# One log/exp table for ScalarE, loaded by hand, and two neighbouring norms taken as one, in a three-block fp32 model on one core

## The reference, cut to what matters

```python
def rmsnorm(x, g):
    return x * lax.rsqrt(jnp.mean(x * x, -1, keepdims=True) + RMS_EPS) * g          # RMS_EPS = 1e-6
def _layer_norm(x, g, b):
    mu = jnp.mean(x, -1, keepdims=True)
    var = jnp.mean(jnp.square(x - mu), -1, keepdims=True)
    return (x - mu) * lax.rsqrt(var + LN_EPS) * g + b                                # LN_EPS = 1e-5

def first_block(x, ...):
    ...                                       # S5 mixer
    out = (y * jax.nn.silu(gate)) @ sgu_w_out[j]
    x = x + out
    return rmsnorm(x, final_g)                # block 1's last norm
def second_block(x, ...):
    h = _layer_norm(x, ln_in_g, ln_in_b)      # block 2's first norm
    proj = h @ w_in[i]
    ...
```

## Time and profile before

| | before |
|---|---|
| median of 3 runs (lowest, highest) | 4123.22 us (4118.02, 4128.06) |
| the profiled execution's own time | 4112.57 us |
| its span | 4110.8 us |
| mean granted TensorE clock | 0.978 |
| TensorE busy (weight loads) | 95% (48%) |
| VectorE, ScalarE, GpSimd busy | 42%, 21%, 14% |
| DMA | 175.02 MB, 43 GB/s on average |

### The profile page before, as it was taken

How to read it: one execution, slowest core, us unless ns; L and a number is a source line. 1 busy time by engine, 2 the same in 40 slices (tenths; PEclk the granted TensorE clock), 3 DMA queues, 4 the chain that set the end, 5 groups by cost and what they waited for, 6 DMA issues and landing times.

```text
span 4110.8 us, 32365 instructions
## 1 busy us (share of the span) xinstructions
PE 3906.0 (95%) x12967; PEld 1982.8 (48%) x12967; DVE 1723.9 (42%) x2515; ACT 882.8 (21%) x1033; POOL 559.8 (14%) x605
## 2 busy tenths in 40 slices
PE   8999999999999999878999999999899999899998
PEld 4554444544345766443444444444355554444554
DVE  8576334333334441244533232323445553424432
ACT  2112111111552212342310000000323420321122
POOL 0343100121002220122111222122000000000000
PEclk9999999999999999999999999999999999999999
DMA  5323111111011110200111111111101001003101
GB/s 144 80 66 88 41 52 41 41 41 41 16 36 42 26 42 19 69 21 14 44 46 41 41 41 51 41 41 41 36 21 32 26 11 47 13 13 100 31 11 51
DMA packets 291233, 175.02 MB, mean 43 GB/s; under 512 B 24103, under 2 KB 281998, under 8 KB 290830
## 3 DMA queue, kind: packets, MB, share of 16 engines
q1 hardware_dynamic: 264736, 132.24, 11.8%
q0 software_dynamic: 9424, 22.30, 2.1%
q10 hardware_dynamic: 16926, 18.43, 1.4%
HBM read 159.72 MB, written 13.21 MB: 42 GB/s over the span
## 4 chain that ended last, share of the span: by engine, by line
PE 55%; ACT 2%; DVE 2%; issue 1%; DMA 0%; POOL 0%; ACTq 0%; DVEq 0%
PE products L326 23%; PE products L2934 8%; PE products L161 7%; PE products L2947 3%; PE others L3013 2%; PE products L2135 1%; PE products L179 1%; PE products L534 1%; PE products L2298 1%; PE others L2329 1%; PE products L2144 1%; PE products L3462 1%; PE products L3461 1%; PE others L1546 1%; PE others L3046 1%
## 5 line engine op out<-in xcount | busy, mean ns | idle before, releaser
L2934 PE MATMUL products<-normed,weights 128*128 128x512 f32 (+2 forms) x704 | 321.6, 607 | 5.0 <-DVE normed L520 5.0
L161 PE MATMUL products<-normed,weights 128*128 128x512 f32 x704 | 309.8, 600 | 8.4 <-DVE s_small L3673 4.0
L326 PE MATMUL products<-gate,s_small 128*128 128x512 f32 x704 | 313.0, 592 | 0.0
L326 PE MATMUL products<-work,s_small 128*128 128x512 f32 x544 | 243.3, 592 | 0.0
L326 PE MATMUL products<-normed,s_small 128*128 128x512 f32 x512 | 230.1, 592 | 2.3 <-DVE row L382 2.3
L344 POOL TENSOR_TENSOR s_small<-weights 128x512 f32<-128x512 f32 x60 | 77.3, 1288 | 1137.6 <-PE products L326 967.0
L356 ACT ACTIVATE s_small<-products 128x512 f32<-128x512 f32 x60 | 35.8, 597 | 860.9 <-PE products L326 860.9
L161 PEld LDWEIGHTS products<-normed,weights 128*128 128x128 f32 x704 | 134.0, 192 | 176.5 <-issue 164.8
L326 PEld LDWEIGHTS products<-gate,s_small 128*128 128x128 f32 x704 | 133.8, 190 | 168.4 <-issue 168.4
L326 PE MATMUL products<-normed,weights 128*128 128x512 f32 x448 | 203.6, 597 | 3.0 <-ACT normed L1077 3.0
L2934 PEld LDWEIGHTS products<-normed,weights 128*128 128x128 f32 (+2 forms) x704 | 126.4, 186 | 164.0 <-issue 162.0
(11 more groups left out here) (594 smaller groups left out, 6119.7 us busy)
## 6 DMA issues: line engine op xcount, KB each, us to landing
weights<-in_w_in_dram SPq DMA_DIRECT2D x83, 512.0 KB, 3.8
weights<-in_w_up_dram SPq DMA_DIRECT2D x32, 512.0 KB, 4.9
weights<-in_w_down_dram SPq DMA_DIRECT2D x32, 512.0 KB, 4.7
weights<-in_sgu_w_in_dram SPq DMA_DIRECT2D x24, 512.0 KB, 5.1
weights<-in_s_w_in_dram SPq DMA_DIRECT2D x16, 512.0 KB, 4.9
weights<-in_w_out_dram SPq DMA_DIRECT2D x24, 256.0 KB, 2.8
branch_scratch<-work POOLq DMA_DIRECT2D x8, 512.0 KB, 3.2
work<-branch_scratch POOLq DMA_DIRECT2D x64, 64.0 KB, 2.6
```

The source lines that it names most:

```text
L161: last = pe.matmul(out[0:cols, half * BANK:(half + 1) * BANK], slot(c, b, kt, cols)[:, k, :], acts[n][:, half * BANK:(half + 1) * BANK], s ...
L326: last = pe.matmul(bank, w[:, k * P:(k + 1) * P], moving[k], start=(k == 0 and n in (1, 3, 5)), stop=(k == KT // 2 - 1), skip_group_check= ...
L2934: last = pe.matmul(out[0:cols, half * BANK:(half + 1) * BANK], slot(c, f.b, kt, cols)[:, kk, :], acts[kk][:, half * BANK:(half + 1) * BANK ...
```

## The change

**By hand.** A class `Scalar` wraps ScalarE's queue. `logs()` loads the set `natural_log_exp_and_others` (set 6, which holds Ln and Exp) unless it is loaded already, and is called at 14 places in the code, most of them ahead of a wait. `activation()` calls it ahead of any Ln or Exp where no place did. For functions outside it (Silu and Sigmoid, for instance) the compiler still puts loads. [...] The program now has 95 loads: 40 of set 6, one of set 5, none of set 0, and the others as before.

**The joined norm.** The RMS norm between the blocks is gone. A class `Weighted` adds up gain times residual for the first seven tiles while the SGU's product is added to the residual (one VectorE pass of 128x1024 for each tile), and VectorE makes two 128x128 matrices: `last_mean`, the mean matrix with its rows scaled by the eighth tile's gain, and `little`, the mean matrix times LN_EPS. The layer norm takes its mean from the total and the eighth tile, subtracts it while it scales (`scalar_tensor_tensor` in place of `tensor_tensor`), and its mean of squares begins with `little` times the sum of the plain squares. `eps_both` is RMS_EPS·LN_EPS; one more constant is set on GpSimd at the start.

```diff
+class Scalar:
+    LOGS = (ACT.Ln, ACT.Exp)
+    ANY = (ACT.Copy, ACT.Identity, ACT.Square, ACT.Abs)
+    def logs(self):
+        if not self.has_logs:
+            self.act.preload_act_table_set("natural_log_exp_and_others")
+        self.has_logs = True
+    def finer_log(self):
+        self.act.preload_act_table_set("natural_log")
+        self.has_logs, self.fine_log = False, True
+    def activation(self, out, source, func, **kw):
+        if func in self.LOGS:
+            if func != ACT.Ln or not self.fine_log:
+                self.logs()
+        elif func not in self.ANY:
+            self.has_logs = False
+        ...
+        return self.act.activation(out, source, func, **kw)
+class Weighted:
+    def matrices(self, dve):
+        c.dve_chain.done(dve.tensor_scalar(self.last_mean, c.mean_mat[:, :], self.gain[:, KT - 1:KT], None, ALU.mult))
+        c.dve_chain.done(dve.tensor_scalar(self.little, c.mean_mat[:, :], LN_EPS, None, ALU.mult))
+    def collect(self, dve, m):
+        c.dve_chain.wait()
+        if m == 0:
+            c.dve_chain.done(dve.tensor_scalar(self.total, c.X[:, m, :], self.gain[:, m:m + 1], None, ALU.mult))
+            return
+        c.dve_chain.done(dve.scalar_tensor_tensor(self.total, c.X[:, m, :], self.gain[:, m:m + 1], self.total, ALU.mult, ALU.add),
+                         c.collected if m == KT - 2 else None)
+    def mean(self, pe, g, last_group):
+        out = start_group(c, pe, g)
+        pe.wait_ge(c.collected, self.collected)
+        ...                                   # 2 matmuls: mean_mat x total
+        taken(c, pe, last_group)
+        ...                                   # 2 matmuls: last_mean x X[7]
+    def before_squares(self, pe, out):
+        pe.wait_ge(sem, value)                # the eighth tile's square
+        ...                                   # 4 matmuls: little x (total of squares, last square)
@@ ln_phase
-            out = start_group(c, pe, g_mean)
-            for k in range(KT):
-                pe.wait_ge(c.normed, after + k + 1)
-                for h in range(HALVES):
-                    last = pe.matmul(out[:, h * BANK:(h + 1) * BANK], c.mean_mat[:, :], src[:, k, h * BANK:(h + 1) * BANK],
-        sum_squares(c, pe, g_sq, *squared)
+            weighted.mean(pe, g_mean, g_mean - 1)
+        sum_squares(c, pe, g_sq, *squared, weighted)
     def scalar(act):
+        act.logs() if weighted is None else act.finer_log()
...
-            ins = dve.tensor_tensor(dst[:, k, :], src[:, k, :], mean, ALU.subtract)
+                ins = dve.scalar_tensor_tensor(dst[:, k, :], src[:, k, :], weighted.gain[:, k:k + 1], mean, ALU.mult, ALU.subtract)
@@ fox_phase
+        act.logs()
         exponentials(0)
@@ residual_sums: collect(m) is sums.collect and then weighted.collect
@@ the program
-        norm = then(rms_phase(c, c.X, c.X, c.vec["final_g"], sums=sgu.sums))
-        norm = then(ln_phase(c, c.X, c.X, c.vec["ln_in_g_2"], c.vec["ln_in_b_2"], after=norm.normed))
+        norm = then(ln_phase(c, c.X, c.X, c.vec["ln_in_g_2"], c.vec["ln_in_b_2"], weighted=sgu.weighted))
```

More of the change, by code:

```diff
@@ L525, in rms_phase, with sum_squares @@
     return phase
-def sum_squares(c, pe, g, ready, used):
+def sum_squares(c, pe, g, ready, used, weighted=None):
     out = start_group(c, pe, g)
+    if weighted is not None:
+        weighted.before_squares(pe, out)
     for k in range(KT):
@@ L534, in sum_squares @@
             last = pe.matmul(out[:, h * BANK:(h + 1) * BANK], c.mean_mat[:, :], c.tmp[:, k % 2, h * BANK:(h + 1) * BANK],
-                             start=(k == 0), stop=(k == KT - 1))
+                             start=(k == 0 and weighted is None), stop=(k == KT - 1))
         last.then_inc(c.square_used if k < KT - 1 else c.group_done, 1)
@@ L551, in next_squares, with ln_phase @@
     return ready, used
-def ln_phase(c, src, dst, gain, bias, means=None, after=None, squares_next=False):
+def ln_phase(c, src, dst, gain, bias, means=None, squares_next=False, weighted=None):
     g_mean = c.plan.groups
@@ L1316, in square_pairs, with residual_sums, collect @@
     squares(len(pairs) - 1)
-def residual_sums(c, dve, pairs, sums, scale=None):
+def residual_sums(c, dve, pairs, sums, scale=None, weighted=None):
+    def collect(m):
+        if m >= 1:
+            sums.collect(dve, m)
+        if weighted is not None and m >= 0:
+            if m == 0:
+                weighted.matrices(dve)
+            weighted.collect(dve, m)
     for i, pair in enumerate(pairs):
         pair.add_all(dve, sums.src[:, 2 * i + 1, :], sums.src[:, 2 * i, :], scale,
-                     *((lambda m=2 * i - 1: sums.collect(dve, m), lambda m=2 * i: sums.collect(dve, m)) if i else ()))
+                     lambda m=2 * i - 1: collect(m), lambda m=2 * i: collect(m))
 def add_to_residual(c, dve, g, sums=None):
@@ L1525, in vector @@
                     ms.make(c, dve, name, a, m_ready)
-        residual_sums(c, dve, outs, sums)
+        residual_sums(c, dve, outs, sums, weighted=weighted)
     phase = Phase(loads=loads, tensor=tensor, scalar=scalar, vector=vector, gpsimd=gpsimd)
-    phase.sums = sums
+    phase.weighted = weighted
     return phase
```

58 lines of the change are left out of this document (51 added, 7 removed).

## The result

| | before | after |
|---|---|---|
| median of the runs (lowest, highest) | 4120.62 us (4110.50, 4128.06) | 4071.23 us (4064.20, 4071.61) |
| span of the profiled execution | 4110.8 us | 4069.6 us |
| mean granted clock | 0.978 | 0.980 |
| TensorE's idle time (span less busy) | 204.8 us | 177.1 us |

The ratio is 0.9875, 95% interval 0.9858 to 0.9892: about 51 us faster. Over all the timings of both kernels in this study (33 executions before, 8 after) the medians are 4121.3 and 4068.4 us, 52.9 apart. Two executions of the study, one of the kernel before (4263.78 us) and one of the variant heads_reload (5903.44 us), had a mean granted clock of 0.928 and 0.646 and are left out. The two profiled executions are only 41.2 apart; why is a question for the experiments.

What follows compares the result with a forecast made beforehand. TensorE, busy 3906.0 of 4110.8 us, was taken as the bound. Loads 27.9, joined norm 22.2, loss −1.3 and clock +3 made 52 us, taken from 4123.2 to give 4071; 8-in-10 range 4052 to 4095.

Steps and rivals of the forecast that it cites:

- (a): Seven norms, from the load phase's to the last: one exposed load less at each, 9.0 us gained.
- (b): Three attention heads and block 3's norms: two exposed loads less at each, 15.1 us together, two block 3 stalls capped at 4.9.
- R1: Rival: VectorE and GpSimd chains set the long stalls at heads and block 3; only 30 us gained, 4093; chance 0.15.
- (c): Block 3's 5.1 us stall at L3013 <- L3194: three loads less in ScalarE's chain, 3.8 us gained.
- (d): Joined norm between the blocks: fewer matmuls and waits, little matmuls covering the first square, one exposed load staying; 22.2 us gained.
- (e): Block 3's small Exp: its load, hidden by a wait before, now stands behind it; 1.3 us lost.
- (f): Half-clock stretches behind long stalls: shorter stalls give some time back, +3 us taken, bounds −6 and +10.
- R3: Rival: shorter stalls no longer end in half-clock stretches; eleven places gain 20.9 us in place of 3, 4053; chance 0.14.
- R2: Rival: a switch costs more than its load's row, exposed parts come back double; 80 us gained, 4043; chance 0.04.
- R4: Rival: the joint set's load is longer; at 5 us each the kernel is 65 us slower, 4188; chance 0.025.
- R5: Rival: nothing moves, the freed time is lost in full to new waits; 4119 or so; chance 0.025.

Runs made afterwards that it cites:

- heads_reload: Changed kernel with two loads (Ln's set, then the joint one) put back at each of the four attention heads' norms: 4089.74 us, ratio 0.9914.
- norm_only: Kernel before with only the joined norm added, the loads left to the compiler (159 loads): 4101.77 us, ratio 0.9947.
- no_little: Changed kernel without the four little matmuls (the LN_EPS times mean square term) ahead of the squares: 4067.36 us, ratio 0.9870.
- joint_ln: Changed kernel with the joint set's logarithm used for the joined norm too: 4064.03 us, ratio 0.9859.
- before_again: Kernel before, no edit, profiled a second time: 4124.16 us in a single execution.
- two_more: Changed kernel with two more loads between Ln and Exp in every inverse_root (152 loads): 4106.53 us, ratio 0.9964.
- on_demand: Changed kernel with every hand-placed joint-set load left to the first Ln or Exp needing it, behind its waits (96 loads): 4077.63 us, ratio 0.9891.
- table_only: Changed kernel with the two norms between the blocks apart as before, so only the load change remains (94 loads): 4084.47 us, ratio 0.9908.
- decay_reload: Changed kernel with the compiler's loads back in block 3's decay phase alone (121 loads): 4089.18 us, ratio 0.9916.
- weighted_first: Changed kernel with the weighted pass ahead of the addition of squares and the load ahead of block 3's small Exp's wait: 4068.76 us, ratio 0.9870.

## Why the prediction was right, point by point

The time came out at 4071.2 against 4071 forecast, closer than the steps behind it deserve: two of them were off and made each other good, and the median of before that it was subtracted from, 4123.2, had become 4120.6. That it came to a fraction of a microsecond is luck.

**(a) One exposed load at seven places: right.** The stalls at L1405 and L2934 went from 5.0 to 3.7, the load phase's from 4.3 to 3.0, the feed-forward's from 8.3 to 7.0 and the last head's from 4.9 to 3.7; the mLSTM's went from 1.5 to 0.2. VectorE's wait ahead of the last norm's scaling fell from 9.07 to 7.78.

**(b) Two loads at the heads: right, slightly more.** VectorE's wait shrank by 2.70 at each of three heads, not 2.56; heads_reload brings it back. R1 is refuted. The two stalls of 2.45 went, but other stalls of 0.7 and 0.9 us at L3110 came next to them, so 3.3 of the 4.9 were gained.

**(c) The chain of three loads: right.** 5.14 became 1.30: 3.84.

**(d) The joined norm: right in place and size.** 22.0 measured between the profiles, 22 in norm_only, 22.2 forecast. One term in it failed: the total's matmuls were to start at once, and waited 1.11 for VectorE's weighted pass (L525). The little matmuls' cover is confirmed by no_little. The tail's one load stayed as forecast, 1.3 us by joint_ln; that this norm's Ln uses a finer set, as the prediction has it, no run shows.

**(e) The loss at block 3's small Exp: right,** 0.6 to 1.9.

**(f) The clock: the step that was mis-sized.** It said "+3", beside 4.7 us of half-clock time that (d)'s sum already holds; the stretch after L578 that (f) names as a gain is part of that 4.7. The two stretches of the earlier trace rows also don't follow their stalls but begin inside them (577.94 and 1011.43, where the stalls end at 580.90 and 1012.24).

Idle time fell by 27.7 us between the first profiles and by 31 between the means of three and of two, where the sum had 34 (27.9 − 1.3, and 7.5 in (d)): too much by the two new stalls at L3110 (1.6), the one at L525 (1.1) and 1.6 more at L2105. The clock made that good. In the decay phase alone it gave 8.6 to 9.3 us of busy time back, in all profiles of both kernels. From the heads' first matmul to the decay phase it gave nothing back: its cost there was 19.2, 28.7 and 19.9 in the three profiles of before, and 30.3 and 30.9 in the changed kernel's. This alone takes 11 us from the difference of the first two profiles, which are 41 apart and not 53. It isn't the loads: norm_only, with the compiler's loads at the heads, had 28.0 there, and the changed kernel's variants 25.1 to 30.8. At the RMS norm before the SGU, the place of the earlier trace rows, the shorter stall changed little: 6.83 us with TensorE busy for 3.9 became 3.41 with TensorE busy throughout, 1.9 and 1.7 of cost.

Over whole executions the medians are 53 apart; 31 of idle time and 10 of matmuls leave some 12 for the clock, an estimate by what is left over, where the prediction had 7.7 (its 3 and the 4.7 in (d)). It has one direct support: before_again, the profile nearest the median of before, had a clock cost 10 above the changed kernel's. The means of the profiles have only 3 (70.2 and 67.2), as two of three profiles of before fell among its quickest executions. R3 had the mechanism, in one phase out of several; its 4053 was not reached.

**R2** is refuted by two_more and joint_ln, and **R4** by 40 loads of the joint set at 1283 ns. R5 did not come either: the time moved by 51 us.

## What to carry to other kernels

Count what an instruction on the waiting chain costs by its row, then ask what the stall does to TensorE's clock behind it: here a microsecond of stall was worth 1.1 us where the heads' loads were put back and 2.0 in the decay phase, and medians moved by still more than twice the idle time where a stretch at half clock came up elsewhere (heads_reload, 18 to 23 us for 6 to 8). When an experiment adds or removes stalls, read idle time and busy time apart, with the number of matmuls beside them; the time alone would have confirmed a wrong price for a load (two_more). A load ahead of a wait that outlasts it is free (at the RMS norm 0.77 us of the wait were left over), one behind the wait costs all of its 1.28 us (on_demand).

## What the runs showed of the hardware that was not expected

A stretch of 20.48 us at half clock in the mLSTM's products in heads_reload and in two_more, with no stall of TensorE in it and one of only 0.17 us in the 45 us ahead of it, and none at that place in the changed kernel, which has the same small wait: some 9 us for nothing that the edit did there. Such a stretch with TensorE busy throughout also stands in the last products of table_only, decay_reload and weighted_first (13.65 us each), and in neither profile of the changed kernel.

And the placing of such stretches repeats: the changed kernel's two profiles agree to 0.1 us in the length of the decay phase (632.15 and 632.08), and those of before and decay_reload to 0.9. Why a stretch falls where it does was not settled.
